# Linear-attention level loop: whole filler projections at three or four levels of a unit in place of half projections at six or eight

## The reference: two kinds of transformer block

```
b = jnp.cumsum(gc, axis=2)
o_inter = jnp.einsum('bhtd,bhdv->bhtv', qc * jnp.exp(b), state)
decay = jnp.exp(jnp.where(causal, b[:, :, :, None, :] - b[:, :, None, :, :], -jnp.inf))
scores = jnp.einsum('bhtd,bhtsd,bhsd->bhts', qc, decay, kc)
o = o_inter + jnp.einsum('bhts,bhsv->bhtv', scores, vc)
```

## Time and profile before

| what | value |
|---|---|
| time, median of 3 runs | 3607.02 us (3604.19 to 3608.08) |
| the profiled execution | 3615.09 us, its span 3613.3 us |
| mean granted clock of PE | 0.945 |
| instructions | 43543 |
| DVE busy | 1470.2 us (41%) |
| ACT busy | 715.7 us (20%) |
| POOL busy | 1942.2 us (54%) |
| DMA | 263.01 MB, mean 73 GB/s |

### The profile page before, as it was taken

One profiled execution on the slowest core, in us unless ns is written; L12 is line 12 of the kernel. 1 busy time (PEld: TensorE's weight loads), 2 busy tenths in 40 slices (PEclk: granted clock), 3 DMA queues, 4 the chain that ended last, 5 costly groups with the idle time before them and its releaser, 6 DMA issues.

```text
span 3613.3 us, 43543 instructions
## 1 busy us (share of the span) xinstructions
PE 3374.3 (93%) x15368; PEld 2610.0 (72%) x15368; DVE 1470.2 (41%) x2456; ACT 715.7 (20%) x1460; POOL 1942.2 (54%) x896
## 2 busy tenths in 40 slices
PE   6899999989999988888999999999888799999998
PEld 5678887768888766664666888877676566678886
DVE  4444421344440366656213544034575532254411
ACT  3310002331000332216211110023221440020101
POOL 3267777337777752310345777776231015467774
PEclk9999999989999998977999999999898699999998
DMA  3122222103222221110122222222111002222221
GB/s 108 42 78 93 95 96 95 59 32 104 93 94 98 82 70 36 42 47 1 53 81 87 96 95 95 93 83 82 36 42 36 24 24 93 79 98 94 95 96 64
DMA packets 71437, 263.01 MB, mean 73 GB/s; under 512 B 7920, under 2 KB 7920, under 8 KB 71152
## 3 DMA queue, kind: packets, MB, share of 16 engines
q1 hardware_dynamic: 71280, 260.98, 21.5%
HBM read 258.85 MB, written 2.10 MB: 72 GB/s over the span
## 4 chain that ended last, share of the span: by engine, by line
PE 61%; POOL 14%; issue 14%; DVE 7%; ACT 3%; POOLq 0%; DMA 0%; DVEq 0%; ACTq 0%; SPq 0%
PE bank L537 60%; POOL w_hi L1195 8%; POOL w_lo L1201 5%; DVE rope L1647 2%; PE bank L1086 1%; DVE arena L1647 1%; ACT arena L1607 1%; DVE arena L2126 0%; DVE arena L1650 0%; ACT arena L1596 0%; ACT act_hi L1326 0%; PE bank L811 0%; ACT rope L1543 0%; DVE rope L2186 0%; ACT arena L1521 0%
## 5 line engine op out<-in xcount | busy, mean ns | idle before, releaser
L1195 POOL TENSOR_TENSOR w_hi<-ring,cst 128x1024 fp32r<-128x1024 f32 (+1 forms) x438 | 834.5, 1905 | 1578.1 <-PE bank L537 1295.7
L1201 POOL TENSOR_TENSOR w_lo<-ring,w_hi 128x1024 fp32r<-128x1024 f32 x430 | 1063.2, 2473 | 33.8
L537 PE MATMUL bank<-h_hi,w_hi 128*128 128x512 f32 x2256 | 918.2, 407 | 2.2 <-DVE h_lo L1674 2.2
L537 PE MATMUL bank<-h_hi,w_lo 128*128 128x512 f32 x2256 | 899.1, 399 | 0.0
L537 PE MATMUL bank<-h_lo,w_hi 128*128 128x512 f32 x2256 | 898.6, 398 | 0.0
L537 PEld LDWEIGHTS bank<-h_hi,w_hi 128*128 128x128 f32 x2256 | 429.2, 190 | 110.1 <-issue 5.2
L537 PEld LDWEIGHTS bank<-h_hi,w_lo 128*128 128x128 f32 x2256 | 429.7, 190 | 106.0
L537 PE MATMUL bank<-act_hi,w_hi 128*128 128x512 f32 (+1 forms) x1296 | 485.6, 406 | 21.9 <-DVE act_hi L2154 7.0
L537 PEld LDWEIGHTS bank<-h_lo,w_hi 128*128 128x128 f32 x2256 | 430.0, 191 | 101.2 <-issue 1.4
L537 PE MATMUL bank<-act_hi,w_lo 128*128 (+1 forms) x1056 | 423.8, 401 | 0.0
L537 PE MATMUL bank<-act_lo,w_hi 128*128 (+1 forms) x816 | 323.5, 396 | 0.0
(11 more groups left out here) (227 smaller groups left out, 3118.7 us busy)
## 6 DMA issues: line engine op xcount, KB each, us to landing
ring<-wstream SPq DMA_DIRECT2D x480, 512.0 KB, 3.4
par<-params SPq DMA_DIRECT2D x5, 656.5 KB, 4.5
x<-xT SPq DMA_DIRECT2D x4, 512.0 KB, 6.4
outT<-h SPq DMA_DIRECT2D x4, 512.0 KB, 2.7
cst<-const SPq DMA_DIRECT2D x1, 1436.5 KB, 10.3
arena<-pos SPq DMA_DIRECT2D x1, 256.0 KB, 10.5
```

What stands on the lines that cost most here:

```text
L537: return pe.matmul(out, lhsT, rhs, start=start, stop=stop)
L1195: return po.tensor_tensor(out, a, C("ones")[:, 0:1].broadcast_to([P, n]), ALU.mult)
L1201: po.tensor_tensor(pair_[1], raw, pair_[0].bitcast(F32), ALU.subtract).then_inc(done.sem, 1)
```

## The change

Fillers are no longer cut in halves. In units 0 to 3 three whole projections follow the scores of levels 1, 4 and 7; in units 4 and 5 four whole projections follow those of levels 1, 3, 5 and 7. The keys and their order are the same, as is all arithmetic. On ACT `landed` follows: the copy of each filler comes one level after the level that holds the projection, now 2, 5, 8 and 2, 4, 6, 8.

```
         FILL = {}
         for u in range(6):
-            levels = (1, 3, 5, 6, 7, 8) if u < 4 else range(1, 9)
+            levels = (1, 4, 7) if u < 4 else (1, 3, 5, 7)
             first = BEFORE + (3 * u if u < 4 else 12 + 4 * (u - 4))
-            FILL |= {(u, v): (YKEYS[first + n // 2], n % 2) for n, v in enumerate(levels)}
+            FILL |= {(u, v): YKEYS[first + n] for n, v in enumerate(levels)}
...
                         if (u, v) in FILL:
-                            project(*FILL[u, v])
+                            project(FILL[u, v])
...
                         if landed is not None:
                             copy_out(landed)
-                        landed = FILL[u, v][0] if (u, v) in FILL and FILL[u, v][1] == 1 else None
+                        landed = FILL.get((u, v))
```

## The result

| | before | after |
|---|---|---|
| median of the runs | 3606.04 us | 3757.91 us (3750.78 to 3769.03, 4 runs) |
| ratio | | 1.0425, 95% interval 1.0404 to 1.0446 |
| profiled execution, span | 3613.3 us | 3749.0 us |
| mean granted clock | 0.945 | 0.927 |

The forecast was 3732 us (3655 to 3775). By medians the change costs 151.9 us where 125.2 were forecast.

What follows compares the result with a forecast made beforehand. PE was taken to wait in the level loop for DVE's k(v) behind projection ends. Per layer, waits 9.6 + 23.6 and slow clock 12.6 + 16.8 make +62.6, over two loops +125.2 us: 3732 us (3655 to 3775).

Steps and rivals of the forecast that it cites:

- E+5: In the level loop, 5 us after a projection's end on PE; the scores two levels on were to start at E+5.1.
- the bound: PE in the level loop rests for DVE's k(v), 22.3 us in 13 waits; each projection end delays scores to E+5.1.
- steps 2 and 3: Behind each projection: scores, no filler, scores; units 4 and 5 cycle in 12.25 us against 9.65, +23.6 us a layer.
- step 1: Whole kernel: no work removed or added; the 20 vanishing joins a layer save 1 us at most, taken as 0.
- steps 3 and 4: Level loop at full clock: units 4 and 5 lose 23.6 us a layer, units 0 to 3 lose 9.6 us.
- step 5: Slow matmuls behind the loop's waits: 12.6 us a layer in units 0 to 3, 16.8 in units 4 and 5.
- signs: In the loop: PE's waits some 75 us, unit 4's cycle 12 to 15 us, k(v+2) 2.6 us, clock under 0.91.
- A: Rival: whole projections keep PE at 2.4 GHz in the loop, 25 us a layer back, 3557 us; chance 0.05.
- B: Rival: the cost in the loop only moves, with S(v+2) ready at the projection's end, 3607 us; chance 0.04.
- C: Rival: between the loop's waits PE never returns to 2.4 GHz, 3887 us; chance 0.03.
- The exclusive port: In the loop, POOL's split locks out DVE's two-input operations; half-speed sharing instead would leave +57 of the +125 us.

Runs made afterwards that it cites:

- short split: The changed kernel with POOL splitting only 256 of the 1024 columns of each weight tile split in the loop: 3599.53 us, ratio 0.9952.
- late copy: The changed kernel with ACT's copy of each filler two levels behind it instead of one: 3593.87 us; the same on the kernel before, with halves: 3572.95 us.
- kernel with PE kept busy: The changed kernel with 2 to 5 matmuls that feed nothing added behind the scores of the level after each filler: 3683.77 us, ratio 1.0189.
- neighbouring levels: The changed kernel with whole fillers at levels 1, 2, 3 (units 0 to 3) and 1, 2, 3, 4 (units 4 and 5): 3674.21 us, ratio 1.0161.

## Why the prediction was right, point by point

- **Scores two levels on at E+5** (the bound, and steps 2 and 3). Right at 17 of the 20 ends of layer 1: 4.94 to 5.06 us, with the releaser named. Two ends have no split and give 1.93 us. The last end of unit 4 gives 6.58 us, because of the silu. The short split and the late copy show that both of its halves are needed, POOL's split and ACT's copy, as the prediction had them.
- **No work changes, joins cost nothing** (step 1). Right: instruction counts are equal. With the late copy, whole fillers are slower than halves by 21 us, so the joins hid no gain of size.
- **Waits at full clock** (steps 3 and 4): 33.2 us a layer, 66 in all, forecast against a before that keeps its slow time. The kernel with PE kept busy gives 67 by medians, 79.9 by its two loops. By units of layer 1: units 0 to 3 +13.2 (9.6 forecast), units 4 and 5 +27.4 (23.6 forecast). The nearness of 27.4 to 23.6 is partly luck: terms that the prediction didn't have cancel. At the last end of unit 4, where the silu now follows a projection, the scores come 1.6 us later than E+5; the prediction had put 1.3 for it in the range only. In unit 5 two ends have no split, which it had not seen; each takes 3 us off, 6 in all. And 6.8 us are the slow `lin_pv` named above, which belong to the clock. Without them the waits of units 4 and 5 cost 20.6 us.
- **The clock** (step 5): 29.4 us a layer forecast, 32.7 and 29.9 measured as the difference of the loops of the changed kernel and the one with PE kept busy (74 for both by medians). The total is right, its parts less so: in units 0 to 3 I took 1.4 us for each of 9 waits on the ground that part of the slow time is absorbed; measured is 18.4, 2.0 each. A third of it, 6.0 us, lies from the last scores of a unit to the next unit, where these scores, those of the next level 0 or `lin_pv` (4.6 us in unit 3, 2.4 before) run slow one behind the other; the other 12.4 us are scores, `lin_sum` and the first matmuls of projections behind the waits inside the units. Part of it is a term that the prediction had at nothing: behind the waits that `lin_pv` partly fills, of 1.76 and 1.04 us in unit 3 and nearly the same in unit 2, 1.5 us each were lost to slow matmuls, while the same pair of waits in unit 1 cost nothing. In units 4 and 5 it is 14.3 against 16.8, for 6 waits and not 8, or 21.1 if the 6.8 us of slow time in the kernel with PE kept busy are counted to the clock.
- **Size.** 125.2 us forecast; 142.5 in the two loops; 141.1 against the later runs of the kernel before, 151.9 by the first medians. The mis-sized terms are the two above for units 0 to 3: together 31.6 us in layer 1 where I had 22.2. Units 4 and 5 gave 41.6 for 40.4, by the cancelling named above. Of the signs, the waits are 69.6 us (some 75 forecast), k(v+2) takes 2.56 us (2.6), and unit 4's second cycle, 15.5 us, lies just outside the 12 to 15.
- **Rivals.** A (whole pieces keep the clock) fell: the loop's clock went from 0.91 to 0.80. The Trainium skill's page "TensorE: Matmul & The Clock Gate", section "Why this matters for your kernels", sets back-to-back matmuls against long waits between them. The change made the rows of matmuls longer, but the waits too, and by the trace these decided: all slow stretches in the projections stand behind waits. B (the cost only moves) fell by the 69.6 us of waits. C (PE never returns to 2.4 GHz) fell in the changed kernel: the projections of units 4 and 5 come back to 0.23 us starts after at most 11 slow ones. Where fillers are gone altogether, behind the neighbouring levels, the clock was 0.64.
- **The exclusive port.** The Trainium skill, page "SBUF — State Buffer", section "SBUF: two separate sides", says that a DVE operation with two SBUF inputs is blocked for the whole of a GpSimd instruction that reads SBUF and started first. All nine traces agree: of some 300 additions and multiplications of two 128x256 SBUF tensors that started well inside one of POOL's instructions, none ended before it. The short split shows the time following POOL's length.

## What to carry to other kernels

When several engines take turns in a fixed order, ask for each long piece of filler not how long it is but what its end sets off, and whether the next piece of filler stands where that is felt. Two delays that cost little alone here (a copy that holds an engine to the end of a product, a split that blocks another engine's multiplications) make one wait when the first pushes work into the second; here moving the copy by one level was worth 164 us with whole fillers and 45 us with halves, and cutting the fillers in halves 21 us once the copy was moved. A stall on the matmul engine had a second price in the slow clock behind it, here at least as large as the stall itself, and it can be measured nearly alone by filling the stall with matmuls that feed nothing.

## What the runs showed of the hardware that was not expected

- Useless matmuls paid: two to five of the helper's products behind a filler took 74 us off a kernel of 3758, and the clock of the loop rose from 0.80 to 0.95.
- A `copy_predicated` with its mask in SBUF and its source in PSUM ran in its usual 0.73 us while POOL was splitting (1491.02, late copy with whole fillers), where multiplications of two SBUF tensors took up to 2.6 us instead of 0.42. The 46 of its kind that ran within one of POOL's instructions in the two kernels with the late copy all took 0.73 or 0.74 us.
